# A second mixer with keys first, rotations inside the projection, and heads turned in two parts

## The reference, cut to what matters

```
shift, scale, gate = adaln(cond, ada_w[l, 0], ada_b[l, 0])
h = rms_norm(x, mix_norm_g[l]) * (1 + scale) + shift
qkv = h @ w_qkv                      # 16 query heads, 4 key heads, 4 value heads of 64
q, k = apply_rope(q, cos, sin), apply_rope(k, cos, sin)
s = einsum(q, k) * 64 ** -0.5;  s = where(|i - j| <= 128, s, -inf)
m = max(max(s), sink);  e = exp(s - m);  p = e / (sum(e) + exp(sink - m))
x = x + gate * ((p @ v) @ w_out)
```

## Time and profile before

| | |
|---|---|
| median of 3 runs | 3010.8 us |
| the profiled execution | 3013.08 us, its span 3011.8 us |
| mean granted PE clock | 0.902 |
| PE busy | 2464.6 us (82%) |
| DVE busy | 1116.5 us (37%) |
| ACT busy | 801.0 us (27%) |
| HBM read | 700.56 MB, mean 233 GB/s |
| DMA in the experts of either layer | 409 GB/s |

### The profile page before, as it was taken

The page is one execution under the profiler, slowest core; times in us unless marked ns, Lnnn a source line. Parts: engine busy times, 40 slices in busy tenths (PEclk is TensorE's granted clock), DMA queues, the critical chain, the costliest instruction groups (busy, mean ns, idle before and its releaser), DMA issues.

```text
span 3011.8 us, 31621 instructions
## 1 busy us (share of the span) xinstructions
PE 2464.6 (82%) x13622; PEld 1565.7 (52%) x13622; DVE 1116.5 (37%) x1667; ACT 801.0 (27%) x1140; POOL 3.2 (0%) x7
## 2 busy tenths in 40 slices
PE   7876656767767767667998888889999998887999
PEld 5542111114443111114988454579889774545897
DVE  3740000003551000003544535565455543456554
ACT  3230000002330000003433322544444332324443
POOL 0000000000000000000000000000000000000000
PEclk9988899888878888888999899999999998998999
DMA  8769999997339999999653233356556432424562
GB/s 310 258 232 409 409 409 409 409 409 284 137 132 390 409 409 409 409 409 281 183 185 125 56 94 117 113 139 182 187 159 182 159 112 71 127 84 126 141 182 97
DMA packets 397104, 703.66 MB, mean 234 GB/s; under 512 B 17187, under 2 KB 232483, under 8 KB 396838
## 3 DMA queue, kind: packets, MB, share of 16 engines
q1 hardware_dynamic: 396966, 701.65, 65.5%
HBM read 700.56 MB, written 1.05 MB: 233 GB/s over the span
## 4 chain that ended last, share of the span: by engine, by line
PE 58%; DMA 24%; DVE 7%; SPq 5%; ACT 4%; issue 1%; DVEq 0%; ACTq 0%
PE psum L688 56%; DMA ring<-in_moe_w_down 9%; DMA ring<-in_moe_w_up 7%; DMA ring<-in_moe_w_gate 7%; SPq L558 5%; PE psum L692 2%; DVE arena L1771 2%; ACT ring L1364 1%; DVE lent_r L1771 1%; ACT lent_r L1364 1%; DVE arena L1779 1%; DVE arena L1782 1%; ACT arena L1364 1%; DMA ring<-in_ada_w 0%; DVE arena_r L1771 0%
## 5 line engine op out<-in xcount | busy, mean ns | idle before, releaser
L688 PE MATMUL psum<-ring,arena 128*32 128x512 f32 (+3 forms) x3672 | 686.0, 665 | 288.5 <-DMA ring<-in_moe_w_up 103.3
L688 PE MATMUL psum<-lent_r 128*128 128x256 f32 (+1 forms) x3440 | 641.7, 300 | 23.8 <-DVE lent_r L1771 23.7
L688 PEld LDWEIGHTS psum<-ring,arena 128*32 128x32 f32 (+2 forms) x3672 | 184.4, 130 | 792.6 <-issue 258.2
L688 PEld LDWEIGHTS psum<-lent_r 128*128 128x128 f32 x3440 | 553.8, 196 | 45.2 <-issue 15.6
L688 PE MATMUL psum<-arena_r,lent_r 128*128 128x256 f32 (+1 forms) x1888 | 520.7, 317 | 16.4 <-DVE lent_r L1771 8.5
L1771 DVE TENSOR_TENSOR lent_r<-ring,lent_r 128x2048 fp32r<-128x2048 f32 (+1 forms) x158 | 349.2, 2211 | 285.6 <-ACT lent_r L1364 285.6
L688 PEld LDWEIGHTS psum<-arena_r,lent_r 128*128 128x128 f32 x1888 | 368.5, 196 | 40.1 <-DVE arena_r L1771 9.8
L1364 ACT ACTIVATE lent_r<-ring 128x2048 fp32r<-128x2048 f32 (+1 forms) x158 | 289.7, 1839 | 160.9 <-PE psum L688 160.5
L1364 ACT ACTIVATE arena<-psum 128x512 f32<-128x512 f32 (+3 forms) x118 | 57.8, 501 | 1017.5 <-PE psum L688 955.0
L688 PE MATMUL psum<-ring,hT 128*128 128x512 f32 (+1 forms) x576 | 271.2, 607 | 3.8 <-ACT arena L1364 2.7
L688 PE MATMUL psum<-lent_r,arena_r 128*128 128x512 f32 x1056 | 241.5, 390 | 0.3
(11 more groups left out here) (140 smaller groups left out, 1519.8 us busy)
## 6 DMA issues: line engine op xcount, KB each, us to landing
ring<-in_moe_w_gate SPq DMA_DIRECT2D x128, 1024.0 KB, 18.5
ring<-in_moe_w_up SPq DMA_DIRECT2D x128, 1024.0 KB, 18.6
ring<-in_moe_w_down SPq DMA_DIRECT2D x128, 1024.0 KB, 18.6
ring<-in_ffn_wi SPq DMA_DIRECT2D x176, 512.0 KB, 5.2
ring<-in_ada_w SPq DMA_DIRECT2D x48, 1024.0 KB, 7.5
ring<-in_w_in SPq DMA_DIRECT2D x46, 1024.0 KB, 5.2
ring<-in_ffn_wo SPq DMA_DIRECT2D x44, 1024.0 KB, 4.9
ring<-in_w_out SPq DMA_DIRECT2D x8, 1024.0 KB, 4.9
```

Source lines behind the costliest of these rows:

```text
L688: return T.matmul(out, lhsT, rhs, start=start, stop=stop, **kw)
```

## The change

Seven edits, all in or for the second mixer, except the masking one, which holds for every attention:
- the angles (DVE), the sines (ACT) and the gate rows of modulation 2 (DVE, PE, ACT) move into group 0 of the experts of layer 0, after the gathers; the wide gate columns stand in `moe[0].y`;
- the keys' and values' columns are projected first, and rotated by DVE while the second chunk is multiplied; the first eight query heads are rotated during the third chunk; `at_.raw` is three buffers;
- PE transposes keys and the first eight query heads, then two steps of modulation 3, then scores of two units; the other eight query heads are rotated and transposed (`other_queries`) behind DVE's first unit, after four steps of modulation 3;
- the exponential table is preloaded on ACT after the projection's cuts;
- masking and maximum are one instruction per head with an accumulator output (`tensor_tensor_reduce`, 256 elements), four per unit;
- the output is split into high and low in four parts, when two units are through (`o_high`, `o_low`), and pieces 6 and 7 of the weights are cut inside the attention (`after`); the first output product waits for its own quarter alone.

The core of the diff:

```diff
-ROPE_STEPS = 6
+ROPE_STEPS, LATE_STEPS = 2, 4
+    at_chunks = [2, 0, 1]
+    at_turns = [8, 9, 10, 11, 0, 1, 2, 3, 4, 5, 6, 7]
# PE, experts, other_rows
+                if layer == 0:
+                    T.wait_ge(*E.spread_v.at(0))
+                    for k in range(KT):
+                        i = mm(psum[:, 4 + k // 4, (k % 4) * P:(k % 4 + 1) * P], wide_gate[:, k, :], ident, True, True)
+                    i.then_inc(*E.spread_p.inc(0))
...
# PE, windowed
+            T.wait_ge(*E.at_dve.at(("rope", 1)))
+            for i in range(8):
+                if i >= 4:
+                    T.wait_ge(*(E.at_odd if i % 2 else E.at_even).at((i - 4) // 2))
+                turn(i, i % 4)
...
+            def other_queries():
+                for _ in range(LATE_STEPS):
+                    next(mod)
+                T.wait_ge(*E.at_dve.at(("rope", 2)))
+                for i in range(8, 12):
+                    if i == 11:
+                        T.wait_ge(*E.at_even.at(4))
+                    turn(i, 4 + (i - 8) % 3)
...
-            T.wait_ge(*E.at_o_low.at(0))
             for p in range(4):
+                T.wait_ge(*E.at_o_low.at(p))
# ACT, experts, group 0 of layer 0
+                if layer + g == 0:
+                    C.wait_ge(*E.spread_p.at(0))
+                    for n in range(2):
+                        af(gates_b[0][:, n * 512:(n + 1) * 512], psum[:, 4 + n, :], ACT.Copy).then_inc(*act.ev(E.gate_out, 2, n))
+                    C.wait_ge(*E.at_dve.at("ang"))
+                    af(at_.sin, at_.ang, ACT.Sin).then_inc(*act.ev(E.at_act, "sin"))
...
# ACT, windowed
+            def after(n):
+                if n % 2 == 0 and n:
+                    o_high(n // 2 - 1)
+                if n in (4, 5):
+                    cut("at", 0, n + 2)
# DVE, attention
-                stt(own, ps, u["scale"], wide(u["mask"], 4), ALU.mult, ALU.add).then_inc(*dve.ev(E.masked, base + n))
+                for j in range(4):
+                    i = V.tensor_tensor_reduce(out=probs[:, j, 0:w], in0=psum[:, banks[j // 2], (j % 2) * S:(j % 2) * S + w],
+                                               in1=u["mask"], scale=u["scale"], scalar=NEG, op0=ALU.add, op1=ALU.max,
+                                               accum_out=st[:, j:j + 1])
+                i.then_inc(*dve.ev(E.masked, base + n))
                 V.wait_ge(*dve.now)
-                alone(red(st[:, 0:4], own, ALU.max))
# DVE, windowed
             for n in range(3):
                 next(pieces)
+                if n:
+                    turns(n - 1)
                 next(pieces)
                 V.wait_ge(*E.qkv.at(2 * n + 1))
...
+            def other_queries():
+                turns(2)
+                for _ in range(LATE_STEPS):
+                    next(mod)
+                for i in (8, 10):
+                    turned(i, 4 + (i - 8) % 3)
+
+            def after(n):
+                if n % 2 and n > 1:
+                    o_low((n - 3) // 2)
+                if n in (6, 7):
+                    cut("at", 0, n)
```

More of the change, by code:

```diff
@@ L948, in experts, with attention @@
                        True, True).then_inc(*E.moe_pe.inc(layer, g, ("back", b)))
-        def attention(units, base, score_banks=((0, 1), (2, 3)), turn_banks=(4, 5), out_bank=6, bufs=None):
+        def attention(units, base, score_banks=((0, 1), (2, 3)), turn_banks=(4, 5), out_bank=6, bufs=None, late=None, after=None):
             turned = {}
@@ L954, in scores @@
                 w = u["keys"] * P
+                for event in u.get("turned", ()):
+                    T.wait_ge(*event)
                 if n >= len(score_banks):
@@ L1547, in attention @@
                 front(u, n)
+                if late and n == 0:
+                    late()
                 yield
@@ L1952, in fourier, with angles @@
             add_gated("fc", 0, 1)
+        def angles():
+            ang, r = at_.ang, at_.r
+            alone(cp(r[:, :, 0], pos_i[:, :]))
+            for t in range(TT):
+                alone(ts(ang[:, t, :], K("inv"), r[:, t, 0:1]))
+            big = 1.5 * 2.0 ** 23
+            alone(ts(r, ang, 1.0 / (2 * math.pi), big, ALU.mult, ALU.add))
+            alone(ts(r, r, -big, op0=ALU.add))
+            c1 = 6.28125
+            c2 = float(np.float32(np.round((2 * math.pi - c1) * 2 ** 20) / 2 ** 20))
+            c3 = 2 * math.pi - c1 - c2
+            for part in (c1, c2, c3):
+                alone(stt(ang, r, -part, ang, ALU.mult, ALU.add))
+            ts(ang, ang, math.pi, -math.pi, ALU.min, ALU.max).then_inc(*dve.ev(E.at_dve, "ang"))
+            V.wait_ge(*dve.now)
+            alone(stt(r, ang, -1.0, ang, ALU.mult, ALU.max))
+            ts(r, r, -1.0, math.pi / 2, ALU.mult, ALU.add).then_inc(*dve.ev(E.at_dve, "abs"))
         def experts(layer, ahead):
@@ new lines, in after, with o_low @@
+            def after(n):
[3 more added lines that the diff above has]
+                    cut("at", 0, n)
+            def o_low(hg):
+                part = slice(2 * hg, 2 * hg + 2)
+                V.wait_ge(*E.at_o_high.at(hg))
+                tt(low[:, part, :], at_.oT[:, part, :], high[:, part, :].bitcast(F32), ALU.subtract).then_inc(*dve.ev(E.at_o_low, hg))
+            weave(mod, 1, (attention(at_units, 0, bufs=at_.bufs, late=other_queries, after=after), 1))
@@ L2160, in windowed @@
             run(mod)
-            V.wait_ge(*E.at_o_high.at(0))
-            tt(low, at_.oT, high.bitcast(F32), ALU.subtract).then_inc(*dve.ev(E.at_o_low, 0))
-            for p in range(6, 10):
+            o_low(3)
+            for p in (8, 9):
                 cut("at", 0, p)
```

179 lines of the change are left out of this document (94 added, 85 removed).

## The result

| | before | after |
|---|---|---|
| median of 4 runs | 3011.1 us | 2980.5 us (2976.1 to 2984.0) |
| profiled execution | 3013.08 us, span 3011.8 | 2984.02 us, span 2982.7 |
| mean granted PE clock | 0.902 | 0.906 |

The ratio is 0.9899, 95% interval 0.9882 to 0.9917; a second set gave 2983.1 against 3011.2 us, 0.9911 (0.9892 to 0.9930). So the change is worth 1.0%, about 30 us. The direction was right, but the time lies 10.5 us under the forecast of 2991 and 5.5 us under the lower end of its range, 2986.

A forecast was written before the change was run, and what follows sets the result against it. The second mixer, alone between two full DMA streams, was taken to hand on its time one to one; gains of 10.35 + 2.1 + 7.1 + 0.7 = 20.3 us took the profiled execution to 2992.8, the median to 2991, range 2986 to 3000.

The forecast's parts named there:

- What bounds the kernel: Second mixer stands alone between two full DMA streams; each us taken out moves all behind it by one us.
- not handed on: Rival, chance 0.03: something other than the mixer's last product holds the second expert stream; gain under 1 us, 3010.
- the sum: Gains of the single edits added: 10.35 + 2.1 + 7.1 + 0.7 = 20.3 us.
- Sines and gate rows ahead: Moved from the second mixer into layer 0's experts: gain 0.7 us in the projection, cost 0 in the experts.
- Rotations inside the projection: Keys and first eight query heads rotated on DVE during the second mixer's projection: no stall; 9 us if paid in full.
- From projection to first masking: Second mixer: 23.7 us falls to 7.6; first masking 16.75 us earlier with the 0.7, bounds 13 to 17.5.
- What goes in between: First masking to PE's start on the first unit's probabilities: 13.8 us instead of 7.4, so 6.4 given back (5 to 9).
- Masking form: Four ops of 256 take 1.83 us instead of 2.52, gain 0.7 per unit, 2.1 over three second-mixer periods (-0.7 to 2.5).
- halved throughput: Rival, chance 0.06: the new masking ops run at half rate, 2.76 us a unit instead of 1.83; about 5 lost, 2996.
- Output halves under the units: Output splits and weight cuts done during attention remove PE's wait before the output product: gain 7.1 us, bounds 4 to 7.1.
- ACT or DVE becomes the bound: Rival, chance 0.12: new cuts in ACT's and DVE's queues limit the second mixer's attention units; 2991 + 7.7 = 2998.
- Later mixers: New masking form in the four other attentions: gain 0.7 us, from one last unit, bounds -1.5 to 1.5.

The follow-up runs named there:

- the second profile of before: The kernel before, unchanged, run and profiled once more: 3011.2 us, 0.9999 against the kernel before; second-mixer stage 164.36 us.
- the undone parts: Kernel after with one part put back each: old masking 2989.7, late output split 2993.3, late rotations 2995.5, sines in mixer 2988.9, heads unsplit 2980.2 us.

## Why the prediction fell short, by its own steps

- **What bounds the kernel:** right. A stage between two full streams hands its time on one to one; the rival "not handed on" is out.
- **The step that failed: the sum took its durations, and the stretches it did not edit, as they stood in the one trace of before, and had no term for PE's level behind a wait.** Work that the forecast held to be unchanged was not: the projection's first products (144 in 34.51, where 12 took 5.46 and 132 took 30.40; 1.35 beside the pause of 0.74), the one-column products (5.71 to 3.63) and the output product (24.7 to 22.1). Together 6.0 of the 11.6 missing in the stage; the last unit's values (2.03 to 1.15) are 0.9 more. The remaining 4.7 are terms of single edits that were mis-sized, below. The windows of the kernel before had the level to read:

```profile
789.00:795.00 6.00, 5.75 (x33) 5.61 (x32) 0.17 (x2) 1.01 (x3) 0.00 (x0) 0.63 0.37 148
...
853.00:856.00 3.00, 2.83 (x7) 2.28 (x8) 2.23 (x2) 0.00 (x0) 0.00 (x0) 0.50 0.00 0
856.00:860.00 4.00, 4.00 (x14) 3.12 (x13) 0.00 (x0) 0.00 (x0) 0.00 (x0) 0.65 0.00 0
860.00:878.00 18.00, 17.84 (x79) 14.45 (x77) 7.92 (x7) 5.97 (x4) 0.00 (x0) 1.00 0.00 1
```

  Seven matmuls in the first 3 us of the output product against about 13 in 3 us further on. Some of it is luck of the execution: the second profile of before has 4.2 us less of it. Against that profile the miss of the stage is 7.4 and not 11.6, and the level is 2.7 of it (0.6, 0.2 and 1.9 in the same three rows). The medians differ by 28 to 31 us and the stages by 27 and 31, so neither profile can be set aside. The Trainium skill describes such a loss in "TensorE: Matmul & The Clock Gate" (section "HAM oscillation — how this bites in real kernels"): where each short piece of matmul work is followed by a wait for data, the next piece starts at the lower rate every time. This case's traces agree: 0.50 behind the pause of 7.08, and 1.00 where idle matmuls reached to 0.99 before the product.
- **Sines and gate rows ahead:** the cost of 0 in the experts was right and with room. The gain of 0.7 was too small: 2.1 against both profiles of before. I had priced the edit by the length of the pause. What the late cut fixed was the start of the second half piece's products, 6.20 us after the first (5.46 and a pause of 0.74 in one profile, 4.72 and 1.48 in the other); without it they start after 4.1. In both profiles the first 3 us run at 0.50, as they do in the kernel after.
- **Rotations inside the projection:** no stall, right (9.0 us hidden; undone, 11.0 lost).
- **From projection to first masking:** 7.6 forecast, 5.8 found. Four pairs were already turned at the end of the projection (754.92), which I had put behind it.
- **What goes in between:** 13.8 forecast, 12.5 found; 0.7 of the difference is twice the masking form.
- **Masking form:** 1.83 forecast from four rows of 0.422 and reads of 0.04; it is 1.48, since the four overlap and the reads lie beside them. (The prediction says that the row of 1.226 includes its accumulator read. That was misread: the read is a row of its own, 0.083, in the kernel before too.) Below the floor of 1.69 that I had given. Per period 0.98 instead of 0.7. The three periods gave 2.0 where 2.1 was forecast, but by luck: the first of them is 5.9 and not 4.77. The estimate by the Trainium skill's formula ("VectorE: DVE Perf Modes", section on the TRN2 errata), 1.70, was nearer but also too high; and against its advice of tiles of 512 or more, merging two passes into ops of 256 won here, 1.48 against 2.52. Of the halved throughput in "Vector Engine (DVE) Microarchitecture Reference" nothing is seen here, where one source is in PSUM: 0.42 per op of 256, as in the earlier trace rows.
- **Output halves under the units:** the pause of 7.1 went, as forecast; 1.0 more is the last unit's masking, which I had cancelled against ACT being late, and the rest the last values at the upper level (1.15 instead of 2.03). The rival "ACT or DVE becomes the bound" is out: the period fell to 4.77.
- **Later mixers, 0.7:** not to be told from their scatter of some 6 us.
- **The range** added bounds of single edits and forgot that unedited work could change with them; all favourable ends together gave 23.6, and 28 to 31 came.

What stays open: the undone parts add up to 38 us (7.6, 11.4, 10.5, 7.1, 1.8) and the whole change is 27 to 31 of stage. The split of heads and the rotations stand in for each other and each brings its own change of PE's level, but no run separates these overlaps. Nor is it shown why the one-column products ran at 0.63 in one execution of the kernel before and at 0.94 in the other, or what decides how long the lower level lasts.

## What to carry to other kernels

Before summing an edit that removes or adds a wait on PE, read the granted clock of the work behind the wait, and price that work at both levels: a pause of 7 us cost 7 and up to 2 more. Where a wait fixes the start of the next work, price the edit by that start and not by the pause's length. Profile the kernel before twice, so that a term of 4 us which comes and goes is known as such. Idle matmuls can recover the level if they stand ahead of the wait and end shortly before what it waits for: with 0.99 and 1.82 us left empty the clock behind was 1.00, with 2.42 left it was 0.66 (single cases, not a limit). Behind the wait they delayed what they were to speed up.

## What the runs showed of the hardware

- Behind a pause of 7.08 us, PE ran at a granted clock of 0.50 for 3 us, then at 0.65 to 0.86 in the 4 us window behind them, and at 1.00 from there on. The 96 matmuls took 24.0 to 24.7 us. Without a pause they took 22.1 where the short groups ahead of them ended at the upper level, and 23.0 to 23.5 where these ended at the lower. With 0.99 us left empty behind idle matmuls they took 22.0, with 2.42 left empty 23.7.
- Successive accumulating DVE operations of 256 elements with one PSUM source start 0.345 us apart though each shows 0.42, and the accumulator reads (0.083) lie under the next operation.
- 40 more idle products (80 instructions, 9.1 us of PE) in a stretch where DMA is full left the stream at 1.03 and 409 to 410 GB/s; SP's queue was 3.0 us late for one matrix, 0.7 at the next, and the time to the last expert product was the same within 0.2 us.
- The same code ran with PE at 0.96 in one profile and at 0.71 in another over the 4.5 us behind its first 3 us, which is worth 1.1 us.
